# Attention over paged keys: sample queries laid out earlier, dropped blocks in four parts, sample scores behind the transposes

## The reference, cut to what matters

```python
s_c = einsum('btgrd,bngd->bgrtn', qg, kc) * scale + bias_c     # compressed blocks of 64 keys
p_c = masked_softmax(s_c, dist_c >= 0)
imp = sum(p_c, axis=2)                                        # over the heads of a group
score = where(forced, 1e4, where(dist_c >= 0, imp, -inf))
top_val, top_idx = top_k(score, 16)                           # 16 blocks are chosen
...
s_s = einsum('btgrd,bgtjd->bgrtj', qg, k_sel) * scale + bias_s # the chosen blocks
s_w = einsum('btgrd,bsgd->bgrts', qg, kw) * scale + bias_w     # a window of 512 keys
o = g0 * o_c + g1 * o_s + g2 * o_w
```

## Time and profile before

| | us |
|---|---|
| three runs | 1643.5, 1646.67, 1649.17 |
| median | 1646.67 |
| the profiled execution | 1646.96 |
| its span, from first to last instruction | 1645.3 |
| its mean granted clock of TensorE | 0.981 |
| PE busy | 1567.4 (95%) |
| DVE busy | 810.0 (49%) |
| POOL busy | 564.3 (34%) |
| ACT busy | 557.2 (34%) |
| attention stage | 234 to 438 |

### The profile page before, as it was taken

The page is one execution under the profiler, slowest core; times in us unless marked ns, Lnnn a source line. Parts: engine busy times, 40 slices in busy tenths (PEclk is TensorE's granted clock), DMA queues, the critical chain, the costliest instruction groups (busy, mean ns, idle before and its releaser), DMA issues. The chain is left out here.

```text
span 1645.3 us, 38857 instructions
## 1 busy us (share of the span) xinstructions
PE 1567.4 (95%) x15766; PEld 1457.6 (89%) x15766; DVE 810.0 (49%) x1354; ACT 557.2 (34%) x1061; POOL 564.3 (34%) x509
## 2 busy tenths in 40 slices
PE   7999988999899999999998999999899999999996
PEld 7999865666699999999998889999799999999995
DVE  4333046666646444443248668776546444343145
ACT  4111034656544222222245333334444222222242
POOL 0001215777433434342024234342034344443012
PEclk9999999999999999999999999999799999999998
DMA  6877979776331222223252324242131222223242
GB/s 205 315 264 240 343 270 385 258 255 229 139 107 39 96 94 92 89 99 106 89 175 99 110 73 144 90 153 93 66 127 40 90 89 89 89 97 120 90 159 88
DMA packets 89282, 238.40 MB, mean 145 GB/s; under 512 B 18509, under 2 KB 21247, under 8 KB 87825
## 3 DMA queue, kind: packets, MB, share of 16 engines
q1 hardware_dynamic: 83832, 222.72, 39.3%
q0 software_dynamic: 2992, 9.71, 1.7%
q10 hardware_dynamic: 2314, 3.96, 0.7%
HBM read 217.81 MB, written 23.77 MB: 147 GB/s over the span
## 5 line engine op out<-in xcount | busy, mean ns | idle before, releaser
L875 DVE TENSOR_TENSOR layer_w_lo<-ring,layer_w_hi 128x1024 fp32r<-128x1024 f32 (+1 forms) x136 | 223.1, 1640 | 259.3 <-ACT layer_w_hi L754 259.3
L1033 PE MATMUL layer_ps<-layer_x_hi,layer_w_hi 128*128 128x260 f32 x1312 | 268.5, 284 | 3.8 <-DVE layer_w_lo L875 2.7
L1033 PE MATMUL layer_ps<-layer_x_hi,layer_w_lo 128*128 128x260 f32 x1312 | 267.7, 284 | 0.0
L1033 PE MATMUL layer_ps<-layer_x_lo,layer_w_hi 128*128 128x260 f32 x1312 | 267.3, 283 | 0.0
L754 ACT ACTIVATE layer_w_hi<-ring 128x1024 fp32r<-128x1024 f32 (+1 forms) x136 | 158.8, 1169 | 206.8 <-PE layer_ps L1033 206.8
L1033 PE MATMUL layer_ps<-layer_h_lo,layer_w_hi 128*128 128x260 f32 x960 | 218.7, 288 | 8.9 <-DVE layer_h_lo L884 8.9
L1033 PEld LDWEIGHTS layer_ps<-layer_x_hi,layer_w_hi 128*128 128x128 f32 x1312 | 204.1, 189 | 5.4 <-DVE layer_w_lo L875 2.9
L1033 PEld LDWEIGHTS layer_ps<-layer_x_hi,layer_w_lo 128*128 128x128 f32 x1312 | 204.2, 189 | 0.0
L1033 PEld LDWEIGHTS layer_ps<-layer_x_lo,layer_w_hi 128*128 128x128 f32 x1312 | 203.5, 189 | 0.1
L1033 PE MATMUL layer_ps<-layer_h_hi,layer_w_hi 128*128 128x260 f32 x704 | 172.8, 286 | 4.9 <-DVE layer_w_lo L875 4.9
L1033 PEld LDWEIGHTS layer_ps<-layer_h_lo,layer_w_hi 128*128 128x128 f32 x960 | 161.9, 193 | 9.5 <-DVE layer_w_lo L880 9.3
(11 more groups left out here) (345 smaller groups left out, 2913.8 us busy)
## 6 DMA issues: line engine op xcount, KB each, us to landing
ring<-in_w_gu SPq DMA_DIRECT2D x88, 512.0 KB, 3.2
ring<-in_w_down SPq DMA_DIRECT2D x48, 704.0 KB, 4.0
ring<-in_hgrn_w_in SPq DMA_DIRECT2D x32, 512.0 KB, 5.5
arena<-in_cache_cmp SPq DMA_DIRECT2D x59, 256.0 KB, 5.8
ring<-in_nsa_w_in SPq DMA_DIRECT2D x21, 512.0 KB, 5.0
kv_slot<-in_slc_kv SPq DMA_DIRECT2D x32, 256.0 KB, 4.6
arena<-in_slc_kv SPq DMA_DIRECT2D x32, 256.0 KB, 4.6
X<-in_slc_kv SPq DMA_DIRECT2D x32, 256.0 KB, 3.8
```

The costliest lines, as they stand in the source:

```text
L875: dve.tensor_tensor(self.w_lo[slot][:, 0:kcs * P], c.ring[:, s, 0:kcs * P], self.w_hi[slot][:, 0:kcs * P].bitcast(F32), ALU.subtract).then ...
L1033: mm = pe.matmul(bank[:, h, 0:TH], wt[slot][:, a], xt[:, x, COLS[h]], start=start and part == 0, stop=stop and part == 2)
```

## The change

The layout of the queries moves from the head of DVE's loop in `attention` to DVE's list in `compress`, behind the copy of the block probabilities; its tile `qz` is now a field of `Attention`, and the wait for it in `blocks_scores` is gone. As the tile lies over projections, the layout waits for their twelve stores. The addition that drops the blocks not chosen is cut in four additions of 128x512, one in each of DVE's steps 4 to 7, behind the copy of line 2100; the first page bank's bias waits for all four. In PE's loop the call of `sample_scores` moves from ahead of the transposes (and of the small product of step 3) to behind them, right ahead of the value products.

```diff
--- before.py
+++ after.py
@@ -1188,6 +1188,7 @@
         self.rows_c = sb("kv_slot", [P, PAGES_A_CHUNK * 512])
         self.T_bias = carve(self.rows_c, NB * 4 * P, 2, 2, SEQ)
         self.Vtok = carve(self.rows_c, NB * 4 * P + 4 * SEQ, TILES, 4 * P)
+        self.qz = carve(HT[:, CK_U:CK_U + 4, :].rearrange("p u t -> p (u t)"), 0, 512)
         self.gT = sb("gT", [P, TILES, 48])
         self.PT = sb("block_probsT", [P, SEQ])
         self.BDv = sb("block_values_diagonal", [P, 8, 2, HD])
@@ -1626,6 +1627,16 @@
             dve.tensor_tensor(S, S, wide(sm), ALU.mult).then_inc(probs, 1)
             dve.wait_ge(turned, 1)
             dve.tensor_copy(at.PT[:, :], b[3][:, :]).then_inc(turned_out, 1)
+            dve.wait_ge(kv_saved, 16 * GATE_U)
+            own.link(dve.memset(at.qz, 0.0))
+            for par in range(2):
+                for g in range(GP):
+                    for g2 in range(2):
+                        rows_g = slice(g2 * HD, (g2 + 1) * HD)
+                        first = par * 80 + g * 40 + g2
+                        own(dve.tensor_scalar(at.qz[rows_g].rearrange("p (q x) -> p q x", q=4)[:, :, first:first + 7:2],
+                                              c.XW[rows_g, g * REP:(g + 1) * REP, SEQ + par:T:2].rearrange("p r q -> p q r"),
+                                              HD ** -0.5, None, ALU.mult))
             dve.wait_ge(second, 3)
             own(dve.tensor_copy(at.kcT[:, :], b[0][:, :]))
             dve.wait_ge(second, 4)
@@ -1638,6 +1649,7 @@
 BANKS = WIN_BANKS + SLC_BANKS
 BLOCKS_TURN = 4
 SLOTS = 4
+DROP_PARTS = 4
 
 
 def bank_turns():
@@ -1667,7 +1679,7 @@
         E = [[carve(arena, 6208 + (h * 4 + j) * SEQ, SEQ) for j in range(4)] for h in range(2)]
         ET = [[carve(arena, 10304 + (h * 3 + j) * SEQ, SEQ) for j in range(3)] for h in range(2)]
         nm, rs, sc = [carve(arena, 13376 + j * 8 * NI, 8 * NI) for j in range(3)]
-        qz, acc_w, O = carve(free, 0, 512), carve(free, 512, 512), carve(free, 1024, 2, 2 * P)
+        qz, acc_w, O = at.qz, carve(free, 512, 512), carve(free, 1024, 2, 2 * P)
         cmpO, par_ident = carve(free, 1536, 2 * P), carve(free, 1792, 2, P)
         acc_s = HT[:, GATE_U, 0:512]
         Ss, Es = [[carve(ring, 4096 + (j * 2 + k) * P, P) for k in range(2)] for j in range(2)]
@@ -1687,7 +1699,7 @@
             ("scores", "biased", "exp", "inverse_sums", "scale_ready", "waited")]
         weighted, turned, turned_out, mixed = [[sem(f"{n}{h}") for h in range(2)] for n in
             ("weighted", "turned", "turned_out", "mixed")]
-        merged, const_in, q_ready = sem("merged"), sem("constants_loaded"), sem("sample_q")
+        merged, const_in = sem("merged"), sem("constants_loaded")
         blocks_scored, blocks_shifted, blocks_exp, blocks_ready, imp_made, imp_read, selected = [sem(f"blocks_{n}") for n in
             ("scored", "shifted", "exp", "probs", "importance", "importance_read", "selected")]
         s_scored, s_biased, s_exp, s_mixed, s_added, s_done, s_turned, s_own = [sem(f"sample_{n}") for n in
@@ -1879,7 +1891,6 @@
 
             def blocks_scores():
 
-                pe.wait_ge(q_ready, 8)
                 sample_products(ps_v, NBLK, lambda b, g: at.kcT[:, b * PAGES * 4:(b + 1) * PAGES * 4]
                                 .rearrange("p (n x) -> p n x", x=4)[:, :, 2 * g:2 * g + 2])
                 sample_products(ps_v[:, NBLK:NBLK + 1], 1, lambda b, g: HT[:, SK_U + g, SEQ + b:SEQ + b + 1])\
@@ -1890,14 +1901,14 @@
                     scores(s)
                 if s == 0:
                     blocks_scores()
-                if s - 1 in bank_of:
-                    sample_scores(bank_of[s - 1])
                 if s == 3:
                     pe.wait_ge(const_in, 64)
                     pe.wait_ge(blocks_ready, 1)
                     pe.matmul(ps_v[:, 64:64 + NBLK], gsum, pc, start=True, stop=True).then_inc(imp_made, 1)
                 if 0 <= s - LAG_T < STEPS:
                     turn(s - LAG_T)
+                if s - 1 in bank_of:
+                    sample_scores(bank_of[s - 1])
                 if s >= LAG_O:
                     mix(s - LAG_O)
             pe.wait_ge(s_done, 1)
@@ -1968,7 +1979,7 @@
                 if n >= 2:
                     dve.wait_ge(s_exp, n - 1)
                 if n == WIN_BANKS:
-                    dve.wait_ge(selected, 1)
+                    dve.wait_ge(selected, DROP_PARTS)
                 start = 3e38 if n == 0 else new_nm[:, :] if n == WIN_BANKS else rows_nm[:, n - 1:n]
                 if n:
                     dve.wait_ge(s_biased, n)
@@ -2001,18 +2012,6 @@
                 own.wait()
                 dve.tensor_copy(cmpO, ps_v[:, 0:2 * P]).then_inc(s_added, 1)
 
-            def sample_queries():
-
-                own.link(dve.memset(qz, 0.0))
-                for par in range(2):
-                    for g in range(GP):
-                        for g2 in range(2):
-                            rows = slice(g2 * HD, (g2 + 1) * HD)
-                            first = par * 80 + g * 40 + g2
-                            dve.tensor_scalar(qz[rows].rearrange("p (q x) -> p q x", q=4)[:, :, first:first + 7:2],
-                                              c.XW[rows, g * REP:(g + 1) * REP, SEQ + par:T:2].rearrange("p r q -> p q r"),
-                                              HD ** -0.5, None, ALU.mult).then_inc(q_ready, 1)
-
             def blocks_first():
 
                 col = PAST + WIN
@@ -2049,8 +2048,13 @@
                     own.link(dve.match_replace(score, top, score, NEG))
 
                 own.link(dve.tensor_scalar(drop, score, FLOOR, NEG, ALU.is_gt, ALU.mult))
-                far = at.bias[:, 0:PAST].rearrange("p (n t) -> p n t", t=BLOCK)
-                dve.tensor_tensor(far, far, drop[:, 0:NBLK].unsqueeze(2).broadcast_to([P, NBLK, BLOCK]), ALU.add)\
+
+            def drop_blocks(part):
+
+                n = NBLK // DROP_PARTS
+                blocks = slice(part * n, (part + 1) * n)
+                far = at.bias[:, 0:PAST].rearrange("p (n t) -> p n t", t=BLOCK)[:, blocks]
+                dve.tensor_tensor(far, far, drop[:, blocks].unsqueeze(2).broadcast_to([P, n, BLOCK]), ALU.add)\
                    .then_inc(selected, 1)
 
             def patch_window():
@@ -2061,8 +2065,6 @@
                                 HT[:, WK_U:WK_U + 2, SEQ:T].rearrange("p g b -> p b g")).then_inc(k_patched, 1)
 
             for s in range(STEPS + LAG_O + 1):
-                if s == 0:
-                    sample_queries()
                 if s < STEPS:
                     u, br, _ = of(s)
                     if s % 6 == 0:
@@ -2104,6 +2106,8 @@
                     blocks_second()
                 if s == 3:
                     blocks_third()
+                if 4 <= s < 4 + DROP_PARTS:
+                    drop_blocks(s - 4)
                 if s == 0:
                     patch_window()
                 if s - 1 in bank_of:
```

## The result

The changed kernel took 1654.24 us (median of 12 runs, 1648.23 to 1659.59), the kernel before, on the same chip, 1646.32 (12 runs, 1641.95 to 1652.18): a ratio of 1.0048, 95% interval 1.003 to 1.0065. A second comparison on another chip gave 1648.91 to 1643.31, 1.0034 (1.0019 to 1.005). So the change makes the kernel slower, by 5.6 to 7.9 us. The forecast was 1649.2, no change, with a range up to 1653.0. The slow side and most mechanisms were right; the sum was too small.

A forecast was written before the change was run, and what follows sets the result against it. PE was taken to bound the attention stage, busy 188.25 of 204 us. From the profiled 1646.96, -0.7 + 0 + 3.25 = +2.5 gave 1649.5, so 1649.2 us for the median; range 1644.3 to 1653.0.

The forecast's parts named there:

- Edit 1: Query layout moved into compression: its 2.1 us on DVE hidden there, PE's 1.36 us idle at the attention head removed.
- D: PE's gain at the head of attention: 1.36 to 4.0 us depending on the clock, 2.7 taken.
- Edit 2: Drop cut in four parts, DVE steps 4 to 7: effect 0 taken, between +0.7 and -1.0 us.
- The rival of the parts that wait for GpSimd: Drop parts of steps 6 and 7 each wait 1.55 us behind a GpSimd multiply: 1649.8 us, chance 0.06.
- Edit 3, steps 13 to 46: Moved sample products expose transposes in steps 19, 22, 34, 37, 46 to waits for DVE's copy: 3.25 us lost.
- all such waits slide along unchanged: Existing idle in steps 12, 24, 27, 39 and before three value products follows PE's own scores; nothing takes back new waits.
- the seams are not dearer by any row: Moving the 20 sample products behind the transposes adds no PE time at the changed neighbours.
- Edit 3, steps 4 and 7: Sample product no longer covers waits before the transposes: 1.0 us later in step 4, about 0.6 in step 7.
- Edit 3, step 10: Bank 4 still arrives at about 279.5; PE waits about 1.1 us, then value products start 0.7 us earlier.
- The head's gain ends here: At step 10 PE's early arrival is lost waiting for bank 4 from memory; only 0.7 us stays gained.
- the stretch from 273 to 277: Second low-clock stretch, some 1.5 us, gone only in the rival of earlier banks: 1640.5 us, chance 0.08.
- the clock falls at step 10: Rival: PE arrives over 2 us early, idles for bank 4, then runs slowly: 3.0 us, 1652.2, chance 0.17.

The follow-up runs named there:

- three traces: The changed kernel unaltered, profiled three times: first execution 1655.76 us, second run 1651.3 us, third run at ratio 1.0034 to the kernel before.
- edits 1 and 2 alone: Changed kernel with sample scores back ahead of the transposes, keeping the moved query layout and four-part drop: 1645.32 us against 1643.85 before, ratio 1.0007.
- edit 3 alone: Kernel before with only the sample scores moved behind the transposes: 1650.44 us, ratio 1.0031.
- Filling the two waits: Bank 3's sample product repeated twice where PE idles in steps 8 and 10: ratio 1.0045 on the changed kernel, 1.0021 on the kernel before.

## Why the prediction was wrong

**Edit 1: right.** The layout is hidden, and the block products wait for nothing. Step 1 starts 1.46 us earlier in all three traces, for the 1.36 of idle time. At the start of step 4 the gain D is 3.4, 2.3 and 2.7 us in the three, as the table counts; 2.7 was taken.

**Edit 2: right, but for 0.44 us in step 44 (below).** The parts take 0.68 us each, and edits 1 and 2 alone measure 1.0007. The rival of the parts that wait for GpSimd did not come. The first two of DVE's parts, the GpSimd multiplies beside them, and of these multiplies the ones that start while a part runs:

```profile
250.48 0.68 DVE L2057 TENSOR_TENSOR sample_bias<-sample_bias,ring 128x512 f32<-128x512 f32 x1
257.49 0.68 DVE L2057 TENSOR_TENSOR sample_bias<-sample_bias,ring 128x512 f32<-128x512 f32 x1
```

```profile
250.05 3.38 POOL L1968 TENSOR_SCALAR arena<-arena 128x128 f32<-128x128 f32 x4 [0.80 <-DVE arena L2090]
256.40 2.89 POOL L1968 TENSOR_SCALAR arena<-arena 128x384 f32<-128x384 f32 x2 [2.96 <-DVE arena L2090]
...
250.64 1.31 POOL L1968 TENSOR_SCALAR arena<-arena 128x256 f32<-128x256 f32 x1
257.62 1.67 POOL L1968 TENSOR_SCALAR arena<-arena 128x384 f32<-128x384 f32 x1
```

The same two shapes in the kernel before:

```profile
255.11 0.92 POOL L1957 TENSOR_SCALAR arena<-arena 128x256 f32<-128x256 f32 x1
258.70 1.24 POOL L1957 TENSOR_SCALAR arena<-arena 128x384 f32<-128x384 f32 x1
```

Each part starts inside a running multiply and is no longer than the price from the earlier trace rows, 0.69: DVE did not wait. GpSimd did: the multiply that starts while a part runs takes 1.31 and 1.67 us instead of 0.92 and 1.24, and beside the other two parts 1.94 and 1.25 instead of 1.56 and 0.92. That is 1.5 us of GpSimd in all, the same in the three traces, and it costs PE nothing that shows: its one wait for GpSimd in the stage, 0.5 us, is there with edit 3 alone too. The Trainium skill ("SBUF — State Buffer", section "Who interferes with whom") would have whichever comes second wait for the other; this trace agrees for the multiplies and not for the parts.

**Edit 3, steps 13 to 46: the mechanism right, the size 0.5 short.** Predicted were five waits of 0.56, 0.63, 0.60, 0.86 and 0.60, 3.25 us. All five came: 0.48, 0.56, 0.53, 0.86 and 0.53, 2.96 us. Step 19 reads, DVE and then PE:

```profile
316.88 0.74 DVE L2004 SCALAR_TENSOR_TENSOR HT<-HT,pa_sample_fade,pa_sample_values 128x512 f32<-128x512 f32 x1
317.54 0.55 DVE L2102 COPY arena<-pa_t 128x384 f32<-128x384 f32 x1
```

```profile
318.24 0.52 PE L1806 MATMUL pa_t<-ident,arena 128*128 128x128 f32 x3 [0.48 <-DVE arena L2102]
```

The copy stands behind the accumulation and ends at 318.09; the transposes start 0.15 later, as reckoned. Two terms were missing. One value product, in step 44, waits 1.25 us for the accumulation instead of 0.81: +0.44, where the prediction had all such waits slide along unchanged. This is not edit 3's: the wait is as long with edits 1 and 2 alone (2.9 us in the list, 2.4 with edit 3 alone). DVE starts the small sum ahead of that accumulation late, with nothing that the profile shows it to wait for:

```profile
418.80 0.30 DVE L2003 SCALAR_TENSOR_TENSOR pa_sample_total<-pa_sample_total,pa_sample_fade,pa_sample_sums 128x1 f32<-128x1 f32 x1 [0.38 <-issue]
```

These 0.38 us stand in all seven traces that have edits 1 and 2 and the accumulation at its old place, and in none of the five without these edits; what DVE does in them stays open. And, with edit 3, PE's busy time in these steps grows by 0.77 (133.56 to 134.33), where "the seams are not dearer by any row". They are in places: directly behind the sample product the product with the block probabilities takes 1.13 us, where the earlier trace rows show 1.02:

```profile
329.88 1.08 PE L1849 MATMUL pa_sample_scores<-arena,HT 128*32 128x128 f32 x32
330.89 1.13 PE L1821 MATMUL pa_o<-block_probsT,block_values_diagonal 128*128 128x512 f32 x2
```

The sum 2.96 + 0.44 + 0.77 is the 4.17 measured; without the 0.44 it is 3.73, and edit 3 alone measured 3.65. That 0.5 is what edit 3 cost beyond the prediction here.

**Edit 3, steps 4 and 7: about right.** Step 4 takes back 2.1 and 1.1 us in the first two traces (1.0 predicted) and 3.3 in the third; the first and the third have low clock there. Step 7 takes 0.45 in each (0.6).

**Edit 3, step 10: this step failed.** "The head's gain ends here", with 0.7 gained behind it, holds for the second trace only (-0.8). The term came out at +0.9, -0.8 and +1.7 in the three traces, +0.6 in the mean. What the prediction took from the queue was right: bank 4 comes at 45.2 us in both traces that wait for it, and the stores hold it. What it left out is that PE is not early by D as a fixed sum, since the granted clock behind PE's waits does not repeat. PE idles 1.8 us in step 8 in every trace of both kernels; in the list of before this is the row

```profile
PE pa_sample_values L1874 <- DVE HT L1993: 1.8, 1, 1.8
```

Before, the granted clock fell to 0.50 behind it: that is the stretch from 273 to 277 that the prediction has in a rival and otherwise takes as given. In the changed kernel's first two traces it did not fall there; PE reached step 10 2.9 and 2.7 us early and idled 1.87 and 1.65 us for bank 4 (0.67 before). In the third it fell there, and PE came 2.2 us late. Behind the wait of step 10 it fell in the first trace and not in the second. The rival "the clock falls at step 10" had this at 3.0 us and only for D near 4; it cost 1.8 (12.6 to 10.8 us from step 9 to 11) with D at 3.4. The Trainium skill ("TensorE: Matmul & The Clock Gate", section "What's actually happening") says of the rise of the clock that its place varies from run to run of one kernel; here the place of the falls does so too, with 3.3, 1.6 and 8.2 us of low clock in the three traces.

**The sum.** -0.7 + 0 + 3.25 = 2.5 was predicted, the stage shows 0.6 + 0.4 + 3.7 = 4.7 in the mean of three traces (step 10; step 44, of edits 1 and 2; the other steps from 13 to 46). That is 0.29%, inside the second comparison's interval (0.19 to 0.50) and just below the first's (0.30 to 0.65). Up to 3 us of the first comparison remain unexplained; the time around the stage scatters by more than that from trace to trace. The forecast "no change" failed by the 2.2 us between 2.5 and 4.7 and by this rest.

## What to carry to other kernels

Work that an engine does between a wait's cause and the wait is cover: before moving it, list for each step when the other engine's copy ends and when this engine is then free, as was done here, and ask whether the copy itself can come earlier (taking the accumulation out of its way made steps 11 to 47 5.6 us shorter). A gain ahead of a transfer is kept only if the transfer's place in its queue moves too, and if no other wait in between takes it; here both had to go together. Where PE waits, as here in steps 8 and 10, a low clock behind the wait belongs into the forecast as a spread, not as a sum.

## What was not expected of the hardware

The same kernel lost, by the estimate of the table, 1.6, 3.3 and 8.2 us at the 1.2 GHz level in one stage; the spread is more than the whole effect of the edits. Filling the two waits kept the granted clock at 1.00 in their steps and changed the stage by no more than 0.1 us in the kernel before. A GpSimd multiply that starts while DVE's addition of 128x512 runs took 0.3 to 0.4 us longer, while the addition, started inside a running multiply, took no longer in the changed kernel (0.68 us) and at most 0.1 longer in any trace.
